# Another pairing of the head-norm sums on TensorE, and three places that follow from it

## The reference

```python
u  = modulate(rms_norm(h, norm_mix[l]), m[3], m[4]) @ w_in[l]       # and the same for the context
ua, ub, ucn, ud = jnp.split(u, MIX_SPLITS, axis=-1)
oa = mla_mixer(ua, ...)      # low-rank q and kv, heads of 64 + 32 (rotary) columns
ob = rwkv_mixer(ub, ...)     # forward and backward scans
on = na_mixer(ucn, ...)      # neighbourhood attention, heads of 64
od = gqa_mixer(ud, ...)      # grouped-query attention, heads of 64, rotary
h = h + m[5] * (jnp.concatenate([oa, ob, on, od], axis=-1) @ w_out[l])
```

```python
def rms_norm(x, gain):
    y = xf * lax.rsqrt(jnp.mean(xf * xf, axis=-1, keepdims=True) + NORM_EPS)
    return y * gain

q, k = rms_norm(q, qn), rms_norm(k, kn)     # over the 64 (or 96) columns of one head
```

## Time and profile before

| | |
|---|---|
| median of 3 runs | 3606.82 us (3600.3 to 3610.38) |
| the profiled execution's own time | 3610.38 us |
| its span, first to last instruction | 3608.6 us |
| PE busy, share of span | 3396.0 us, 94% |
| PEld busy | 2899.5 us, 80% |
| DVE busy | 1881.9 us, 52% |
| ACT busy | 1154.9 us, 32% |
| POOL busy | 402.7 us, 11% |
| mean granted TensorE clock | 0.972 of full speed |
| the block of `qkv`, first and second layer, in the trace | 811 to 853 us and 2700 to 2744 us |

### The profile page before, as it was taken

The page is one execution under the profiler, slowest core; times in us unless marked ns, Lnnn a source line. Parts: engine busy times, 40 slices in busy tenths (PEclk is TensorE's granted clock), DMA queues, the critical chain, the costliest instruction groups (busy, mean ns, idle before and its releaser), DMA issues. The chain is left out here.

```text
span 3608.6 us, 68342 instructions
## 1 busy us (share of the span) xinstructions
PE 3396.0 (94%) x28396; PEld 2899.5 (80%) x28396; DVE 1881.9 (52%) x2891; ACT 1154.9 (32%) x1700; POOL 402.7 (11%) x274
## 2 busy tenths in 40 slices
PE   6999999999878899999999999999999878889999
PEld 5888888885657778888888888888885667779897
DVE  4552554665764555543554552554645655555353
ACT  3321322226642133322222321222236532144231
POOL 2000002005113211000001000002006123120000
PEclk8999999999989999999999999999999989899999
DMA  5221221430000012221221221221430000022222
GB/s 194 95 100 64 87 98 67 145 134 30 1 17 3 3 47 83 87 94 69 99 86 64 96 101 63 87 98 67 151 106 7 17 2 3 14 76 87 94 93 93
DMA packets 68260, 263.45 MB, mean 73 GB/s; under 512 B 7536, under 2 KB 8688, under 8 KB 67440
## 3 DMA queue, kind: packets, MB, share of 16 engines
q1 hardware_dynamic: 67648, 256.95, 20.8%
q10 hardware_dynamic: 432, 3.88, 0.3%
HBM read 258.70 MB, written 2.10 MB: 72 GB/s over the span
## 5 line engine op out<-in xcount | busy, mean ns | idle before, releaser
L240 PE MATMUL ps<-hn_hi,w_hi 128*128 128x512 f32 (+1 forms) x3520 | 872.7, 329 | 19.4 <-DVE hn_lo L447 5.9
L240 PE MATMUL ps<-hn_hi,w_lo 128*128 128x512 f32 (+1 forms) x3520 | 873.0, 329 | 0.0
L240 PE MATMUL ps<-hn_lo,w_hi 128*128 128x512 f32 (+1 forms) x3520 | 868.4, 328 | 0.0
L217 ACT ACTIVATE w_hi<-raw 128x1024 fp32r<-128x1024 f32 (+1 forms) x300 | 338.5, 1128 | 1343.8 <-PE ps L240 1175.3
L222 DVE TENSOR_TENSOR w_lo<-raw,w_hi 128x1024 fp32r<-128x1024 f32 (+1 forms) x300 | 396.8, 1322 | 521.8 <-ACT w_hi L217 514.3
L240 PEld LDWEIGHTS ps<-hn_hi,w_hi 128*128 128x128 f32 x3520 | 547.4, 189 | 88.3 <-issue 22.9
L240 PEld LDWEIGHTS ps<-hn_lo,w_hi 128*128 128x128 f32 x3520 | 547.9, 190 | 61.3
L240 PEld LDWEIGHTS ps<-hn_hi,w_lo 128*128 128x128 f32 x3520 | 544.3, 189 | 61.1
L240 PE MATMUL ps<-g_hi,w_hi 128*128 128x512 f32 (+1 forms) x1424 | 398.2, 347 | 6.8 <-DVE g_lo L881 6.8
L240 PE MATMUL ps<-g_lo,w_hi 128*128 128x512 f32 (+1 forms) x1424 | 403.8, 351 | 0.0
L240 PE MATMUL ps<-g_hi,w_lo 128*128 128x512 f32 (+1 forms) x1424 | 398.5, 347 | 0.0
(11 more groups left out here) (266 smaller groups left out, 4231.7 us busy)
## 6 DMA issues: line engine op xcount, KB each, us to landing
raw<-wgu SPq DMA_DIRECT2D x176, 512.0 KB, 3.5
w_mod_one<-wmod SPq DMA_DIRECT2D x109, 512.0 KB, 3.4
raw<-wdn SPq DMA_DIRECT2D x64, 704.0 KB, 4.1
raw<-win SPq DMA_DIRECT2D x44, 512.0 KB, 5.5
w_mod_two<-wmod SPq DMA_DIRECT2D x19, 512.0 KB, 6.0
raw<-wout SPq DMA_DIRECT2D x16, 512.0 KB, 3.4
w_mod_first<-wmod_first SPq DMA_DIRECT2D x2, 2048.0 KB, 18.7
w_mod_first<-wmod_first SPq DMA_DIRECT2D x1, 4096.0 KB, 30.2
```

What stands on the lines that cost most here:

```text
L217: act.activation(w_hi[s][:, 0:kt, :].rearrange("p k n -> p (k n)"), raw[s][:, 0:kt * P], ACT.Copy).then_inc(hi_ready[s].sem, 1)
L240: mm = pe.matmul(out[:, o:o + b - a], w[:, k, :], m[:, k, a:b], start=(k == 0 and w is w_hi[s] and m is mov_hi), stop=(k == kt - 1 and w i ...
```

## The change

The full diff:

```diff
@@ qkv, tables
-        H_QN, H_QG, H_QM, N_STAT = 0, 4, 32, 64
+        H_QN, H_QM, H_QG, N_STAT = 0, 32, 36, 64
...
-            SQUARES = ("kv", "gk", "nk0", "nk1", "kr", "qr", "qn0", "kn0", "kn1", "gq0", "gq1", "nq0", "mq0", "nq1", "mq1", "qn1")
-            SUMMED = ("kv", "gk", "kr", "nk0", "kn0", "nk1", "kn1", "gq0", "qr", "gq1", "qn0", "nq0", "mq0", "nq1", "mq1", "qn1")
+            SQUARES = ("kv", "gk", "nk0", "nk1", "kr", "qr", "qn0", "kn0", "kn1", "gq0", "gq1", "nq0", "nq1", "mq0", "mq1", "qn1")
+            SUMMED = ("kv", "gk", "nk0", "nk1", "kr", "kn0", "kn1", "gq0", "gq1", "qr", "qn0", "nq0", "nq1", "mq0", "mq1", "qn1")
@@ qkv, ACT
                     for j in range(2):
                         square(f"nq{j}", u[:, U_NQ + j, :])
+                    k_heads(0)
+                    for j in range(2):
                         square(f"mq{j}", u[:, U_QC + j, :])
-                    for j in range(2):
-                        k_heads(j)
+                    k_heads(1)
                     q_nope(1, U_QN1, 5)
@@ qkv, PE
                     SUMS = {"kr": (0, four_sel), "kn0": (0, pair_sel(0)), "kn1": (0, pair_sel(2)),
                             "nk0": (1, pair_sel(0)), "nk1": (1, pair_sel(2)), "gk": (1, pair_sel(4)),
-                            "nq0": (2, pair_sel(0)), "nq1": (2, pair_sel(2)), "gq0": (2, pair_sel(4)), "gq1": (2, pair_sel(6)),
-                            "qr": (3, four_sel), "qn0": (3, pair_sel(0)), "qn1": (3, pair_sel(2)), "mq0": (3, share_sel), "mq1": (3, share_sel)}
+                            "nq0": (2, pair_sel(0)), "nq1": (2, pair_sel(2)),
+                            "qr": (3, four_sel), "qn0": (3, pair_sel(0)), "qn1": (3, pair_sel(2)), "gq0": (3, pair_sel(4)),
+                            "gq1": (3, pair_sel(6)), "mq0": (3, share_sel), "mq1": (3, share_sel)}
...
-                    sums("gk", "kr")
-                    sums("nk0", "kn0")
+                    sums("gk", "nk0")
+                    sums("nk1", "kr")
                     rotate("kr", K_["rot_m"], u[:, U_KR, :])
-                    sums("nk1", "kn1")
+                    sums("kn0", "kn1")
                     rotate("gk", K_["rot_g"], u[:, U_GK, :])
-                    sums("gq0", "qr")
+                    sums("gq0", "gq1")
                     pe.wait_ge(head_rstd_ready.sem, head_rstd_ready.at(2))
                     spread(0, "spread_a")
-                    sums("gq1", "qn0")
+                    sums("qr", "qn0")
                     spread(1, "spread_b")
-                    sums("nq0", "mq0")
+                    sums("nq0", "nq1")
                     spread(2, "spread_c")
                     project(U_QN1, (128, 512), (U_QC, U_QC + 1))
                     rotate("qr", K_["rot_m"], q_rope)
-                    sums("nq1", "mq1")
                     rotate("gq0", K_["rot_g"], u[:, U_GQ, :])
-                    sums("qn1")
+                    sums("mq0", "mq1")
                     pe.wait_ge(mla_gained.sem, mla_gained.at(4))
                     values(U_V0, 0)
                     rotate("gq1", K_["rot_g"], u[:, U_GQ + 1, :])
+                    sums("qn1")
                     values(U_V1, 3)
```

## The result

The changed kernel takes 3626.34 us (median of 5 runs, 3623.92 to 3629.09) against 3606.82: a ratio of 1.0056, 95% interval 1.0041 to 1.0070, or 20 us more (15 to 25). The forecast was 3624 and +17.4. The profiled execution took 3625.68 us with a span of 3623.9.

What follows compares the result with a forecast made beforehand. PE's own program was taken to set the block's length. 7.68 + 1.0 = 8.7 us a layer, 17.4 in both, on the median 3606.8 gave 3624.2, say 3624; range 3614 to 3635.

Steps and rivals of the forecast that it cites:

- The six calls in series: PE's sums: in six calls now in one quarter the second tile adds 1.28 us each, 7.68 us a layer.
- The upper bound, open weight loads: Rival for the six calls: weight loads stand open, 5.3 us a layer more, 10.6 in all, 3634.8; chance 0.06.
- The order at PE's end: PE's reordered calls near the block's end: changes of shape cost 0, at most 0.2 us a layer either way.
- ACT's moved copies: Key copies on ACT, moved behind the first scaled keys: PE's wait on them is covered by 8.4 us, cost zero.
- The wait at the end: PE ahead of `turn(3)`: late `qn1` sums delay ACT's chain, adding 1.0 us a layer, bounds 0 to 2.
- the clock as a few us either way: Stages behind the block: clock shifts a few us; giving back much 0.03, taking 5 to 10 us more 0.02.

Runs made afterwards that it cites:

- this part alone: Changed kernel with PE's last calls in the old order, so only the six one-quarter calls remain: stretch 39.94 us in both layers, ratio 1.0043 to the kernel before.
- the new end alone: Kernel before with PE's last calls in the new order and nothing else: stretch 33.68 and 33.52 us, ratio 1.0018 to the kernel before.
- the query copies early: Changed kernel with ACT's four rotary query copies ahead of the query factors: stretch 39.85 and 39.84 us, ratio 1.0038 to the kernel before.
- the same pairs over two quarters: Changed kernel with `gq0` in quarter 2 and `nq1` in quarter 3, so two calls span two quarters again: 38.40 and 38.29 us, ratio 1.0031 to the kernel before.
- the loops exchanged: Kernel before with the two loops in `sums` exchanged, both spans of one tile before the next tile: stretch 32.30 us in both layers, ratio 1.0001.
- the two kernels built to tell three and not four: Kernel before with its first two calls each in one quarter, loops as before or exchanged: 4.42 and 3.99 us for both calls, stretches 33.96 and 33.57.

## Why the prediction was right

**The six calls in series.** Sized at 1.28 us each, 7.68 a layer; measured 7.70 with this part alone. The upper bound, open weight loads, is out: a call in one quarter takes 2.70 us, not 3.5. The sentence cited for it from the Trainium skill, "TensorE: Matmul & The Clock Gate", section "Part 3: Packing small matmuls — row/col tiling", does not by itself hold for these products: all use the same rows, and their loads of 0.11 us lie inside the beat of 0.43.

**The order at PE's end.** The changes of shape cost nothing net, as said: between `qr`'s rotation and the first turns the second layer of the kernel with the new end alone takes 8.38 us (2728.35 to 2736.73), as before (838.71 to 847.09).

**ACT's moved copies.** No wait of PE on them appears, as said.

**The wait at the end.** Sized at 1.0 us, measured 0.95; ACT's own wait was put at 2.5 and is 2.44. With 7.70 that makes 8.65 for the first layer, which grew by 8.62. One reading was not quite right: PE had a second idle gap in this block before, 0.17 us at 848.41, for DVE's copy of the values; the changed kernel hasn't it, and it matters to no term. The experiments with the end alone and with the query copies early show where the wait comes from: `qn1` late, then ACT's chain, then the slot of `turn(1)`.

**What the forecast missed.** No term of the sum stood for the clock around the end of the block. The block was put at 40.9 us in both layers; the second took 41.84, because `turn(3)` to attention took 3.50 us there instead of 2.52, and attention opened at half pace in both. PE in order of time at attention's start, the kernel before:

```profile
858.75 5.46 PE L1394 MATMUL ps<-k_mla,q_mla 96*128 96x512 f32 x8 [2.60 <-ACT probs L1453]
...
866.81 2.82 PE L1394 MATMUL ps<-k_mla,q_mla 96*128 96x512 f32 x8 [0.29 <-ACT probs L1453]
```

and the changed kernel:

```profile
868.62 5.22 PE L1396 MATMUL ps<-k_mla,q_mla 96*128 96x512 f32 x8 [2.58 <-ACT probs L1455]
...
876.43 2.82 PE L1396 MATMUL ps<-k_mla,q_mla 96*128 96x512 f32 x8 [0.52 <-ACT probs L1455]
```

From attention's first product to its third group of scores it takes 13.48 us before (853.33 to 866.81) and 15.85 after (860.58 to 876.43); in the second layer 13.49 and 16.00. The clock fell in both kernels, one group later before. So +2.4 and +2.5 us at attention's starts and +1.0 at the turns of the second layer can be seen in the profile, 5.9 in all. The prediction had the clock as a few us either way, and gave only 0.02 to its taking 5 to 10.

Against this, the profiled spans differ outside the two blocks by -2.9 us (-1.37 + 0.42 - 1.97) with attention's starts in it, so the rest is 7.8 us shorter. Part of that is chance: the profiled execution of the kernel before was 3.6 us above its median. The median is 2 us above the forecast; with an interval of 15 to 25 us neither a net cost of the clock nor its absence is shown by the runs. That the whole came so close is in part luck: the two terms of the block are right to 0.05 us, while 5.9 us that the sum left out and 7.8 the other way, noise with it, offset each other.

## What to carry to other kernels

Float32 products with 32 output columns over all 128 rows cost the same one, two or three at a time if they write different quarters of the partitions (1.41, 1.42 and 1.42 us a call here), and add up in full if they write the same one (2.70 for two). Put neighbours in different quarters, and count the tiles of each quarter, since they follow one another. When a short engine wait is moved into a dense stretch of matmuls, look at the products that come behind it as well as at the wait. And follow the last reduction of a block (here the sums of `qn1`) through the other engine's queue and back: moving it by two calls cost a wait of 1 us on PE.

## What the runs showed of the hardware that was not expected

- A matmul record can start ahead of records that wait for another quarter. It passed three waiting ones with the loops exchanged, and in the two kernels built to tell three and not four: 4.42 us and 3.99 us follow from that count. Each record has a weight load of its own, so whether the count is of matmul records or of instructions stays open.
- Attention's first eight records, by kernel, first and second layer: with the wait of 0.95 us ahead of `turn(3)` 5.46 and 5.46 (the changed kernel), 4.96 and 5.12 (only the end), 5.38 and 5.46 (the same pairs over two quarters). Without it 2.82 in thirteen of fourteen passes of seven kernels, and 4.51 in one. So the 0.95 us of idle PE go with the fall of the clock ahead of attention, six passes of six; the one pass without it shows that they are not needed for it. These are one profile of each kernel. Up to attention's third group of scores it takes 14.6 to 16.0 us with the wait, and without it 11.2 to 13.5, in that one pass 15.2.
